# Root of the RMS norms from the raw sum on ScalarE, transposed chunks in bank c mod 4, first output piece on the sync engine's queue

## What is computed

```python
h = rmsnorm(x, ln_mix_g); proj = h @ w_in            # lru_x | lru_gate | q | k | v
y_lru  = rg_lru(conv4(lru_x)) * gelu(lru_gate)       # gates: sigmoid of 64x64 block products
y_attn = causal attention, 8 heads of 64             # SEQ is one block of 256
x = x + concat(rmsnorm(y_lru), rmsnorm(y_attn)) @ w_out
x = x + cross_attention(rmsnorm(x, ln_cross_g), rmsnorm(mem, ln_mem_g))
t = rmsnorm(x, ln_ffn_g); q = t @ peer_wq            # 8 heads, two halves of 128
ids, gates = product-key top 16 of 128 x 128 experts per head
y[t] = sum_e gates[t,e] * gelu(t . u[ids[t,e]]) * v[ids[t,e]]
out = rmsnorm(x + y, ln_final_g)                     # rmsnorm(a, g) = a / sqrt(mean(a*a) + 1e-6) * g
```

## Time and profile before

| what | value |
|---|---|
| median of 3 runs | 975.21 us (974.95 to 975.78) |
| profiled execution, its own time | 973.53 us |
| span of that execution, first to last instruction | 971.6 us |
| PE busy | 961.6 us, 99% of the span |
| DVE, ACT, POOL busy | 790.6, 550.5, 486.8 us |
| mean granted TensorE clock | 0.998 |
| last norm's root to the last store issued | 965.84 to 968.52 us |

### The profile page before, as it was taken

The page is one execution under the profiler, slowest core; times in us unless marked ns, Lnnn a source line. Parts: engine busy times, 40 slices in busy tenths (PEclk is TensorE's granted clock), DMA queues, the critical chain, the costliest instruction groups (busy, mean ns, idle before and its releaser), DMA issues.

```text
span 971.6 us, 18460 instructions
## 1 busy us (share of the span) xinstructions
PE 961.6 (99%) x7031; PEld 931.1 (96%) x7031; DVE 790.6 (81%) x1546; ACT 550.5 (57%) x979; POOL 486.8 (50%) x315
## 2 busy tenths in 40 slices
PE   8999999999999999999999999999999999999997
PEld 8999899999999999999998888889999999999997
DVE  5858666455999999999988787777899899999896
ACT  7786556546555646464555575555555555555556
POOL 1000001001388888888888888827388873313310
PEclk9999999999999999999999999999999999999999
DMA  9689764624638787778778877879999999999991
GB/s 317 216 301 339 247 226 157 204 88 138 210 60 202 171 213 182 208 177 198 208 189 209 195 177 187 205 208 309 330 360 351 327 361 367 351 352 371 372 331 65
DMA packets 134107, 235.12 MB, mean 242 GB/s; under 512 B 38592, under 2 KB 87488, under 8 KB 133664
## 3 DMA queue, kind: packets, MB, share of 16 engines
q1 hardware_dynamic: 97392, 208.14, 64.2%
q0 software_dynamic: 36224, 25.70, 13.9%
q10 hardware_dynamic: 432, 0.57, 0.2%
HBM read 216.38 MB, written 17.97 MB: 241 GB/s over the span
## 4 chain that ended last, share of the span: by engine, by line
PE 97%; ACT 1%; DVE 1%; DMA 0%; issue 0%; ACTq 0%; DVEq 0%
PE acc L1399 23%; PE acc L1655 11%; PE bank L1655 11%; PE bank L1620 9%; PE bank L1589 8%; PE bank L1588 8%; PE bank L1590 8%; PE bank L1656 5%; PE acc L1656 5%; PE bank L1621 5%; PE bank L1573 1%; PE bank L1497 1%; PE bank L1364 1%; PE bank L1519 1%; PE bank L1428 0%; DMA xr<-x 0%
## 5 line engine op out<-in xcount | busy, mean ns | idle before, releaser
L468 POOL DMA_INDIRECT wmap<-gate,widx x192 | 319.1, 1662 | 90.3 <-issue 59.2
L750 ACT ACTIVATE hl<-raw 128x1024 fp32r<-128x1024 f32 x192 | 202.9, 1058 | 84.4 <-DMA raw<-v 30.4
L1120 DVE TENSOR_TENSOR hl<-raw,hl 128x1024 fp32r<-128x1024 f32 x99 | 121.0, 1223 | 25.2 <-ACT hl L750 22.8
L491 POOL DMA_INDIRECT vg<-v,idx_v x48 | 76.9, 1602 | 118.1 <-DVE acc_s L1261 97.8
L1588 PE MATMUL bank<-xt,hl 128*128 128x256 f32 x480 | 135.9, 283 | 0.0
L1589 PE MATMUL bank<-xt,hl 128*128 128x256 f32 x480 | 135.8, 283 | 0.0
L1590 PE MATMUL bank<-xt,hl 128*128 128x256 f32 x480 | 135.7, 283 | 0.0
L1127 DVE TENSOR_TENSOR hl<-raw,hl 128x512 fp32r<-128x512 f32 x186 | 119.4, 688 | 17.0 <-ACT hl L750 14.2
L1655 PE MATMUL acc<-whl,hl 128*128 128x416 f32 x380 | 121.4, 370 | 0.0
L1655 PE MATMUL bank<-whl,hl 128*128 128x416 f32 x380 | 120.9, 368 | 0.0
L1399 PE MATMUL acc<-xt,wsp 128*128 128x256 f32 x960 | 119.1, 284 | 0.1
(11 more groups left out here) (292 smaller groups left out, 2253.8 us busy)
## 6 DMA issues: line engine op xcount, KB each, us to landing
raw<-u_t SPq DMA_DIRECT2D x128, 512.0 KB
raw<-v SPq DMA_DIRECT2D x128, 512.0 KB
wmap<-zeros SPq DMA_DIRECT2D x6, 2048.0 KB, 11.8
wblk<-wmap SPq DMA_DIRECT2D x62, 192.0 KB
wraw<-w_in SPq DMA_DIRECT2D x9, 1024.0 KB, 9.4
wraw<-w_pq SPq DMA_DIRECT2D x8, 1024.0 KB, 5.2
wraw<-w_ck SPq DMA_DIRECT2D x4, 1024.0 KB, 7.9
wraw<-w_cv SPq DMA_DIRECT2D x4, 1024.0 KB, 7.5
```

Of the source, the lines that this page charges most:

```text
L468: nc.gpsimd.indirect_dma_start(out=wmap, out_offset=bass.IndirectOffsetOnAxis(ap=set_ranks(widx, k)[:, h, r:r + 1], axis=0), in_=set_ranks ...
L750: nc.scalar.activation(eslot(k, 0, second), raw[:, k // 2, k % 2], ACT.Copy).then_inc(ready, 1)
L1120: V.tensor_tensor(eslot(k, 1, second), raw[:, k // 2, k % 2], eslot(k, 0, second).bitcast(F32), ALU.subtract).then_inc(ready, 1)
```

## The change

Three edits. (1) For norms 0 and 1 ACT takes the root directly of the accumulated sum, with scale 1/D and EPS from a constant column as added rest, once its own squares are there. For norms 2 and 3 DVE sums the first three quarters of both tiles beforehand and forms (that sum)/D + EPS (`three_quarters`); ACT takes the root of the fourth quarter's sum with scale 1/D and this rest added. (2) Chunk c of the transposes goes to bank c mod 4. `t_high` waits for its bank's transposes for c < 4, and from c = 4 on for `t_low` of chunk c - 4; `t_low` of a chunk waits for `t_high` of that chunk alone. (3) The first half of output rows 0 to 127 is stored by SP ahead of its other two pieces; ACT writes both halves and then stores the second.

```diff
--- before.py
+++ after.py
@@ -190,7 +190,7 @@
         ND = 32
         SP = 48
         QS = 96
-        WARM = 104
+        WARM, EPSC = 104, 110
         GS = 72
         s_par, s_mem, s_bd, s_keys, s_xd, s_xr2, s_out = (sem(n) for n in (
             "s_par", "s_mem", "s_bd", "s_keys", "s_residual_stored", "s_residual_back", "s_out"))
@@ -405,12 +405,14 @@
                     sp.dma_start(flat(xr2[:]), xres).then_inc(s_xr2, 16)
                 if j % 2 and (j + 3) // 2 < NWB:
                     weights((j + 3) // 2)
+            sp.wait_ge(s_fina, 1)
+            sp.dma_start(out[0:P, 0:512], orow[:, 0, 0:512]).then_inc(s_out, 16)
             for k in range(2):
                 sp.wait_ge(s_fin, k + 1)
                 q = slice(512 * k, 512 * k + 512)
                 sp.dma_start(out[P:2 * P, q], orow[:, 1, q]).then_inc(s_out, 16)
-            sp.wait_ge(s_out, 16 * 2)
-            sp.wait_ge(s_outa, 16 * 2)
+            sp.wait_ge(s_out, 16 * 3)
+            sp.wait_ge(s_outa, 16)
 
 
         @block.gpsimd
@@ -519,9 +521,14 @@
                 nc.scalar.activation(stat[:, WARM + 1:WARM + 2], stat[:, WARM:WARM + 1], ACT.Sqrt)
 
             def tile_deviation(n, t):
-                act.wait_ge(s_var, norm_count(n, t))
-                nc.scalar.activation(stat[:, RS + 2 * n + t:RS + 2 * n + t + 1], stat[:, SS + 2 * n + t:SS + 2 * n + t + 1],
-                                     ACT.Sqrt).then_inc(s_std, 1)
+                if n < 2:
+                    act.wait_ge(s_sq, TT * n + t + 1)
+                    ss, rest = stat[:, SS + 2 * n + t:SS + 2 * n + t + 1], stat[:, EPSC:EPSC + 1]
+                else:
+                    act.wait_ge(s_sq, 2 * TT + 5 * (n - 2) + 3 + t + 1)
+                    act.wait_ge(s_var, n)
+                    ss, rest = stat[:, QS + 4 * t + 3:QS + 4 * t + 4], stat[:, SS + 2 * n + t:SS + 2 * n + t + 1]
+                nc.scalar.activation(stat[:, RS + 2 * n + t:RS + 2 * n + t + 1], ss, ACT.Sqrt, scale=1.0 / D, bias=rest).then_inc(s_std, 1)
 
             def squares(n, t, src, junk):
                 nc.scalar.activation(junk[:, t], src[:, t], ACT.Square,
@@ -533,9 +540,11 @@
 
             def t_high(k, gain, dst, c0=0, c1=DC):
                 for c in range(c0, c1):
-                    if c % 2 == 0:
-                        act.wait_ge(s_tr, 4 * k + c // 2 + 1)
-                    nc.scalar.activation(dst[:, c, 0], bank[c // 2][:, T * (c % 2):T * (c % 2) + T], ACT.Copy,
+                    if c < 4:
+                        act.wait_ge(s_tr, 4 * k + c + 1)
+                    else:
+                        act.wait_ge(s_tl, DC * k + c - 3)
+                    nc.scalar.activation(dst[:, c, 0], bank[c % 4][:, T * (c // 4):T * (c // 4) + T], ACT.Copy,
                                          scale=pcol(gain, c)).then_inc(s_th, 1)
 
             def unit_dst(u):
@@ -555,7 +564,7 @@
                         return f(dst, u0)
 
             nc.scalar.dma_start(pars[:], par).then_inc(s_par, 16)
-            act.wait_ge(s_warm, 1)
+            act.wait_ge(s_warm, 2)
             warm_sqrt()
             for t in range(TT):
                 act.wait_ge(s_x[t], 16)
@@ -655,7 +664,7 @@
             for c in (2, 3):
                 head_group(c)
             unit(U_OUT - 1)
-            act.wait_ge(s_var, 5)
+            act.wait_ge(s_var, 1)
             nc.scalar.activation(stat[:, RS + 12:RS + 16], stat[:, SS + 12:SS + 16], ACT.Sqrt).then_inc(s_std, 1)
 
             def residual_units(u0, n):
@@ -861,8 +870,8 @@
                 act.wait_ge(s_ft, 2 * k + 1)
                 q = slice(512 * k, 512 * k + 512)
                 nc.scalar.activation(orow[:, 0, q], acc[:, 2 + k], ACT.Copy, scale=fin_rec[:, 0:1]).then_inc(s_fina, 1)
-                act.wait_ge(s_fina, k + 1)
-                act.dma_start(out[0:P, q], orow[:, 0, q]).then_inc(s_outa, 16)
+            act.wait_ge(s_fina, 2)
+            act.dma_start(out[0:P, 512:D], orow[:, 0, 512:D]).then_inc(s_outa, 16)
 
 
         @block.vector
@@ -886,11 +895,6 @@
 
             def tile_norm(n, t, src, dst):
 
-                dve.wait_ge(s_sq, TT * n + t + 1 if n < 2 else 2 * TT + 5 * (n - 2) + 3 + t + 1)
-                ss = stat[:, SS + 2 * n + t:SS + 2 * n + t + 1]
-                if n >= 2:
-                    link(V.tensor_reduce(ss, stat[:, QS + 4 * t:QS + 4 * t + 4], X, ALU.add))
-                V.tensor_scalar(ss, ss, 1.0 / D, EPS, ALU.mult, ALU.add).then_inc(s_var, 1)
                 dve.wait_ge(s_std, norm_count(n, t))
                 rd = stat[:, RS + 2 * n + t:RS + 2 * n + t + 1]
                 if (n, t) in ACT_SCALED:
@@ -901,11 +905,12 @@
 
             def t_low(k, gain, dst, c0=0, c1=DC):
                 for c in range(c0, c1):
-                    dve.wait_ge(s_th, DC * k + c + 2 - c % 2)
-                    V.scalar_tensor_tensor(dst[:, c, 1], bank[c // 2][:, T * (c % 2):T * (c % 2) + T], pcol(gain, c),
+                    dve.wait_ge(s_th, DC * k + c + 1)
+                    V.scalar_tensor_tensor(dst[:, c, 1], bank[c % 4][:, T * (c // 4):T * (c // 4) + T], pcol(gain, c),
                                            dst[:, c, 0].bitcast(F32), ALU.mult, ALU.subtract).then_inc(s_tl, 1)
 
             V.memset(stat[:, WARM:WARM + 1], 1.0).then_inc(s_warm, 1)
+            V.memset(stat[:, EPSC:EPSC + 1], EPS).then_inc(s_warm, 1)
             for t in range(TT):
                 tile_norm(0, t, xr, xs)
 
@@ -1066,6 +1071,12 @@
                 xc = xr[:, t, c0:c0 + WCOL]
                 return V.tensor_tensor(xc, acc[:, 2 * (u % 2) + t, 0:WCOL], xc, ALU.add)
 
+            def three_quarters(n):
+                dve.wait_ge(s_sq, 2 * TT + 5 * (n - 2) + 3)
+                part = stat[:, SS + 2 * n:SS + 2 * n + TT]
+                link(V.tensor_reduce(part, stat[:, QS:QS + 4 * TT].rearrange("p (t q) -> p t q", q=4)[:, :, 0:3], X, ALU.add))
+                V.tensor_scalar(part, part, 1.0 / D, EPS, ALU.mult, ALU.add).then_inc(s_var, 1)
+
             def residual_units(u0, n, residual):
                 for u in range(u0, u0 + 3):
                     dve.wait_ge(s_wmm, u + 1)
@@ -1075,6 +1086,7 @@
                         unit(u)
                 dve.wait_ge(s_t0, n - 1)
                 residual(u0 + 3, 0).then_inc(s_res, 1)
+                three_quarters(n)
                 tile_norm(n, 0, xr, xs)
                 dve.wait_ge(s_wmm, u0 + 4)
                 residual(u0 + 3, 1).then_inc(s_res, 1)
@@ -1359,10 +1371,10 @@
 
                 for t in range(TT):
                     pe.wait_ge(s_xs, TT * n + t + 1)
-                    for c in range(DC):
-                        o = T * (c % 2) + P * t
-                        last = pe.transpose(bank[c // 2][:, o:o + P], src[:, t, P * c:P * c + P], ident[:])
-                        if t == 1 and c % 2:
+                    for c in (0, 4, 1, 5, 2, 6, 3, 7):
+                        o = T * (c // 4) + P * t
+                        last = pe.transpose(bank[c % 4][:, o:o + P], src[:, t, P * c:P * c + P], ident[:])
+                        if t == 1 and c >= 4:
                             last.then_inc(s_tr, 1)
 
             def unit(u, xin, fresh=None, part=(0, DC)):
```

## The result

The changed kernel takes 978.23 us (median of 17) against 975.33 for the kernel before on the same chips: ratio 1.0036, interval 1.0027 to 1.0045. It is slower, and outside my range of 973.4 to 976.8. Its profiled execution has a span of 975.3 us, 3.7 above the 971.6 of before.

A forecast was written before the change was run, and what follows sets the result against it. PE, busy for all but 10 us of the span, was taken as the bound, so edits count only where it waits. Terms -0.38 + 1.25 - 0.19 - 0.67 + 0 = +0.01 gave 975.2 us, range 973.4 to 976.8.

The forecast's parts named there:

- What costs nothing: All norms: added DVE sum instructions (0.16 and 0.15 us) hide in 0.57 idle; root stays 0.20; transposes and memset cost nothing.
- -0.67: Norm 3: root 0.38 us earlier, last low part 0.67 earlier, so PE gains 0.67; bounds 0.38 and 0.75.
- this rival: PE's clock falls in the new wait before unit 4, costing 5.9 us for that unit alone; 981 us, chance 0.05.
- Start: Norm 0: earlier roots and low part let unit 0 begin 0.38 us earlier; bounds 0.30 and 0.6.
- The wait at norm 1: Norm 1: t_high waits for t_low behind DVE's convolution, so unit 4 begins 1.25 us later; bounds 1.1 and 1.7.
- The rival that it would not reach PE: Norm 1: the new wait does not reach PE, leaving -1.24 us; 974.0 us, chance 0.08.
- The table load: Norm 1, ACT: load takes 1.28 us without the skill's 1.38 drain; rival that it costs more: 976.5 us, chance 0.04.
- Norm 2: Norm 2: tile 1's root comes earlier and PE's 0.19 us wait goes, gaining 0.19; bounds 0 and 0.2.
- Stores: End: no gain, DMA at full share; bounds -0.38 and +0.2 us; rival that they gain 0.38: 974.8 us, chance 0.10.
- Scatters: After the norms: later work moves along with PE; rival that a transfer or POOL's scatters set the pace: 976.5 us, 0.08.

The follow-up runs named there:

- experiment 1: Changed kernel with the sum of three quarters scaled one column at a time (two 128x1 instructions, not one 128x2): 975.47 us, ratio 0.9999 to the kernel before.
- experiment 2: Kernel before plus one spare 128x2 scale-and-add on DVE in norm 3, which nobody reads: 978.28 us, ratio 1.0033 to the kernel before.
- experiment 7: Changed kernel with the low part of unit U_PQ made by DVE, so GpSimd is idle in norm 3: 976.23 us, ratio 1.0008 to the kernel before.
- experiment 8: Changed kernel with the same two-column sum as scalar_tensor_tensor, EPS from a second tensor of two columns: 975.38 us, one execution.
- experiment 5: Changed kernel without the 8 scatters of the last head of tile 1: 976.59 us, ratio 1.0018 to the whole kernel before.
- experiment 10: Changed kernel with one-column scaling, old bank layout for norm 1 alone, and 8 scatters left out: 972.33 us.
- experiment 3: Changed kernel with the transposes' old bank layout and waits, roots and stores as changed: 975.62 us, ratio 1.0011 to the kernel before.
- experiment 4: Changed kernel with one-column scaling and the old bank layout and waits for norm 1 alone: 972.80 us, ratio 0.9981 to the kernel before.
- experiment 9: Kernel before with 8 scatters left out, plus the store edit alone: 973.39 us.
- experiment 6: Kernel before without the 8 scatters of the last head of tile 1: 973.46 us, ratio 0.9990 to the whole kernel before.

## Why the prediction was wrong

- **The step that failed** is in "What costs nothing": that the sum of three quarters is two DVE instructions "like L892 and L893, 0.16 and 0.15", hidden in 0.57 of idle time. The first was (0.15). The second was not like L893: L893 had one column, the new one has two, and beside GpSimd's subtraction it took 3.29 [experiments 1, 2, 7]. I had costed it at its price and cover, and never asked what ran on GpSimd at that moment. The row was there to be found: in the trace of before the subtraction runs from 221.31 to 225.94, and DVE's sum of tile 0 lies within it. In place of -0.67 norm 3 gave +2.24 - 0.66 = +1.58. This row of the kernel before, from its timeline of GpSimd, is the one to look for:

```profile
221.31 4.63 POOL L455 TENSOR_TENSOR wsp<-wraw,wsp 128x2048 fp32r<-128x2048 f32 x1 [59.28 <-ACT wsp L501]
```

- **The size of the loss after it.** PE's offset is 2.24 at unit(U_PQ) in the profile of the change and 2.01 at the last root in that of experiment 8. The rest of the 2.9 between the medians goes with the clock; a fall cost about 1.1 where it can be read from two profiles (experiments 5 and 8). How often it falls I infer from the mean clock of each execution. A mean of 0.998 does not tell: the clock also falls once PE's work is done, in the profile of before from about 968.4 to the end, and that alone gives its mean of 0.998. A mean of 0.997 or less does tell. None of the 76 executions of the kernel before beside the experiments has it; nine of the 17 of the changed kernel do, and so do five of nine in experiment 2, which has the gap of norm 3 too, and none of twelve in experiment 1, which has not. So I take it that the clock falls after the new gap in at least half of the executions; only the profiled ones show it directly. One of ten in experiment 10 (975.96) is at 0.997 as well, though its profile has no wait over 0.86 in norm 3; why is open. In profiles the fall was seen in experiments 2, 3 and 5; in those of the change and of experiment 8 the clock stayed at 1.00. I had this rival, but at the wrong gap: I placed it before unit 4, where 1.20 of idleness left the clock at 1.00 in each profile that has it, and priced it at 5.9 at least for a whole unit.
- **Start** right in mechanism and size: -0.39. Half of it did not last: the profile of the change has norm 1's transposes only 0.22 earlier (21.95 against 22.17), and by unit 4 experiments 3 and 4 keep 0.21 and 0.18. Experiment 3, with the old banks, gained only 0.24 at unit 0 (10.39) and kept it, so what did not last is the part that the new layout gave. I take it that the low parts then come no faster than PE uses them; no run tests that.
- **The wait at norm 1** right in place and size: 1.16 between experiment 3 and the changed kernel, 1.25 predicted. It was `t_high`'s wait for `t_low` behind the convolution. The rival that it would not reach PE fell.
- **The table load** took 1.28 and the next instruction began 1.30 after its start, also on the path. The rule of the Trainium skill ("ScalarE: Activation LUTs", What ACT_TABLE_LOAD costs) on an added drain of 1.38 is not what this trace shows.
- **Norm 2**: -0.19 predicted, -0.19 in experiment 4 (0.37 - 0.18).
- **Norm 3 without the stall**: the term -0.67 measured -0.55 (experiments 1 and 4, from U_CQ to U_PQ). I took the root at 0.20; with scale and added rest from SBUF it takes 0.29, and the reciprocal starts 0.10 later behind it (0.33 after the root's start, 0.23 before).
- **Stores** 0, right; the median gives 0.07 (experiment 9). The last issue moved by 0.28 and not by 0.38, as it became SP's.
- **Scatters.** I said that POOL's work moves along with PE. It does, but its chain is as long as PE's u keys, so its jitter reaches PE in either kernel (experiments 5, 6). It explains the spread and the last 1.5 of the profiled span, not the difference of the medians.

On the cause itself the Trainium skill has a rule that I read too late ("Advanced Engine Details and Errata", VectorE Performance Modes): the second SBUF port of VectorE is shared with GpSimd, and instructions of GpSimd and two-port instructions of VectorE block each other. The trace agrees, with 3.29 against 0.17. What the runs show is which instructions were held and until when; that it is a port, or in which mode an instruction runs, they do not show.

## What to carry to other kernels

Price a small VectorE instruction by what GpSimd does at that moment, not by its size: two columns instead of one turned 0.15 us into 3.3. Batching two scalars into one instruction is such a change. And when an interlock between two engines is added to a helper, look up every caller: in one of four norms the other engine had 5 us of other work queued in front.

## What the runs showed of the hardware

- A VectorE instruction of 128x2 from SBUF to SBUF, in a form with one tensor and with two, waited for the end of a running GpSimd subtraction of 4.6 us and ended 0.01 to 0.04 us after it (3.29, 3.47, 3.27 us); with 128x1 it did not (0.22 for two).
- TensorE's clock stayed at 2.4 GHz through gaps of 1.15 and 1.20 us; after gaps of 2.15 to 2.25 it fell in three profiles (experiments 2, 3, 5), for 3.4 us each, and stayed in two (the change, experiment 8).
- A root with scale and an added column from SBUF takes 0.29 us on one column, 0.20 without them.
